# The retention state loop of a hybrid decoder step: four value-row buffers, another order of DMAs, constants behind two weight slots

## The reference

```python
def retention_chunk(S, q, k, v, log_gamma):      # for a sample: L = 1
    ...
    cross = jnp.einsum('bihd,bhdv->bihv', q * q_dec[None, :, :, None], S)
    ...
    S_new = jnp.exp(L * log_gamma)[None, :, None, None] * S + jnp.einsum('bjhd,bjhv->bhdv', k * k_dec[None, :, :, None], v)
    return inner + cross, S_new
```

## Time and profile before

| | |
|---|---|
| median of 3 runs | 1556.37 us (1551.08 to 1560.65) |
| the profiled execution | 1557.63 us, its span 1555.7 us |
| TensorE busy | 1378.6 us, 89% of the span |
| VectorE busy | 636.5 us, 41% |
| ScalarE busy | 248.1 us, 16% |
| POOL busy | 122.0 us, 8% |
| granted TensorE clock, mean | 0.91 of full speed |

### The profile page before, as it was taken

One profiled execution on the slowest core, in us unless ns is written; L12 is line 12 of the kernel. 1 busy time (PEld: TensorE's weight loads), 2 busy tenths in 40 slices (PEclk: granted clock), 3 DMA queues, 4 the chain that ended last, 5 costly groups with the idle time before them and its releaser, 6 DMA issues.

```text
span 1555.7 us, 19005 instructions
## 1 busy us (share of the span) xinstructions
PE 1378.6 (89%) x6290; PEld 753.3 (48%) x6290; DVE 636.5 (41%) x1681; ACT 248.1 (16%) x518; POOL 122.0 (8%) x234
## 2 busy tenths in 40 slices
PE   6899876789998999999899969988888889999995
PEld 4687544567864443334577723322324644334343
DVE  2132334320025444444400087787781243535354
ACT  2001224312013000000210021221221130000001
POOL 3331223210000000000000001111110000000000
PEclk9899978899999999999899956686799989999998
DMA  9764848686566999999953346666663639999992
GB/s 373 296 232 151 287 175 258 238 267 264 194 275 234 388 402 399 401 408 406 396 214 128 136 157 214 220 244 229 234 240 136 237 142 353 407 393 416 400 405 111
DMA packets 77033, 430.16 MB, mean 277 GB/s; under 512 B 9833, under 2 KB 11129, under 8 KB 38433
## 3 DMA queue, kind: packets, MB, share of 16 engines
q1 hardware_dynamic: 52704, 347.72, 57.1%
q0 software_dynamic: 23200, 76.10, 14.6%
q10 hardware_dynamic: 1056, 5.36, 0.9%
HBM read 406.94 MB, written 22.20 MB: 276 GB/s over the span
## 4 chain that ended last, share of the span: by engine, by line
PE 69%; DMA 14%; DVE 9%; issue 3%; ACT 2%; DVEq 1%; POOL 1%; SPq 0%; POOLq 0%; ACTq 0%
PE bank L802 66%; DMA ring<-wstream 7%; DMA xn<-v_rows 4%; DMA arena<-state 2%; DVE arena L2163 1%; DVE arena L1999 1%; DVE h L2159 1%; PE bank L858 1%; DVE x L2015 1%; DVEq L1994 1%; DVE arena L1721 1%; ACT arena L1530 1%; ACT xn L1418 1%; DVE arena L2028 1%; POOL ss_out L715 0%
## 5 line engine op out<-in xcount | busy, mean ns | idle before, releaser
L802 PE MATMUL bank<-arena 128*128 128x264 f32 (+7 forms) x1216 | 407.0, 526 | 60.4 <-DVE arena L1721 32.2
L802 PE MATMUL bank<-ring,arena 128*64 128x512 f32 (+3 forms) x1856 | 393.0, 558 | 9.1 <-issue 5.8
L802 PEld LDWEIGHTS bank<-arena 128*128 128x128 f32 (+4 forms) x1216 | 171.7, 169 | 275.4 <-issue 169.0
L802 PEld LDWEIGHTS bank<-ring,arena 128*64 128x64 f32 (+3 forms) x1856 | 141.7, 137 | 240.6 <-issue 208.1
L1400 ACT ACTIVATE arena<-bank 128x256 f32<-128x256 f32 (+6 forms) x186 | 87.0, 472 | 555.6 <-PE bank L802 456.4
L802 PE MATMUL bank<-h,ring 128*128 128x264 f32 x640 | 149.0, 395 | 6.3 <-DMA ring<-wstream 6.3
L802 PEld LDWEIGHTS bank<-h,ring 128*128 128x128 f32 x640 | 123.9, 195 | 32.5 <-issue 11.1
L2015 DVE SCALAR_TENSOR_TENSOR x<-bank,mod,x 128x256 f32<-128x256 f32 x256 | 119.2, 472 | 0.0
L802 PE MATMUL bank<-arena,ring 128*128 128x264 f32 x512 | 116.3, 390 | 0.8 <-DVE arena L2242 0.8
L802 PE MATMUL bank<-arena,cst 16*128 16x128 f32 (+8 forms) x210 | 78.1, 481 | 32.9 <-DVE arena L2224 20.3
L802 PEld LDWEIGHTS bank<-arena,ring 128*128 128x128 f32 x512 | 98.2, 192 | 18.3 <-DVE arena L2242 0.9
(11 more groups left out here) (229 smaller groups left out, 868.2 us busy)
## 6 DMA issues: line engine op xcount, KB each, us to landing
ring<-wstream SPq DMA_DIRECT2D x296, 1024.0 KB, 8.7
arena<-vcache POOLq DMA_DIRECT2D x64, 512.0 KB, 5.6
arena<-kcache SPq DMA_DIRECT2D x64, 512.0 KB, 4.7
arena<-state POOLq DMA_DIRECT2D x32, 512.0 KB, 8.8
ss_out<-arena POOLq DMA_DIRECT2D x32, 512.0 KB, 7.7
xn<-v_rows POOLq DMA_DIRECT2D x32, 256.0 KB, 7.7
sp_out<-arena ACTq DMA_DIRECT2D x4, 512.0 KB, 2.9
cst<-consts SPq DMA_DIRECT2D x1, 2005.5 KB, 16.4
```

The source lines that it names most:

```text
L802: ins = nc.tensor.matmul(out, w, rhs, start=start, stop=stop, skip_group_check=True)
```

## The change

- The value rows get a fourth buffer. The four now take 2048 of the columns of `xn` from its start; `vpart`, which lay there, moves to `sp_sb`.
- POOL's loop goes pair by pair. It waits until VectorE has moved pair p, spreads the rows of units 2p + 4 and 2p + 5, waits until TensorE has read the pair, stores its two units, and loads the states of units 2p + 3 and 2p + 4 (where these are 7 or more). The next head's values are stored after the second of four pairs, as before.
- ScalarE scales pairs in that order: sample_rows(0) takes the place of scale_pair(5) behind v column 7; in head hd the two scalings are of pairs 5 + 2hd and 6 + 2hd (they were 6 + 2hd and 7 + 2hd); sample_rows(2) stands in front of the second scaling of head 3 and not behind it; pairs 13, 14 and 15 follow g columns 0, 1 and 2 (14 and 15 followed columns 0 and 1).
- SyncE loads slots 12 and 13, the first two of q, before the rest of the constants.
- POOL's first seven state loads wait for VectorE's first rotated q column and not for the first row of m0b.

```diff
@@ -376,7 +376,6 @@
         ret = Region(0)
         qk = ret.take(2 * KT, T)
         vtok = ret.take(2, RH * RV)
-        vpart = xn[:, :, :].rearrange("p a b -> p (a b)")[:, 0:RV]
         qz = ret.take(2, RH, NS * NS)
         oret = ret.take(RVT, T)
         gsil = ret.take(2, 2, T)
@@ -386,12 +385,13 @@
         at_sb = ret.take(2, 3 * P)
         ktok = ret.take(2, 2, RK)
         sp_sb = ret.take(2, RV)
+        vpart = sp_sb.rearrange("p a b -> p (a b)")[:, 0:RV]
         sq_s = ktok.rearrange("p a b c -> p (a b c)")[:, 0:RVT * NS].rearrange("p (t b) -> p t b", t=RVT)
         rot = ret.take(4, T)
         osb = rot.rearrange("p a b -> p (a b)")[:, RV:2 * RV]
         root_o = ret.take(1, TP)
         vr = rot.rearrange("p a b -> p (a b)")[:, 0:RV]
-        vb = xn[:, :, :].rearrange("p a b -> p (a b)")[:, RV:4 * RV].rearrange("p (r n) -> p r n", r=3)
+        vb = xn[:, :, :].rearrange("p a b -> p (a b)")[:, 0:4 * RV].rearrange("p (r n) -> p r n", r=4)
         squares = gsil.rearrange("p a b n -> p (a b) n")[:, :, 0:TP]
         hs = oret.rearrange("p a b -> p (a b)")[:, 2304:2304 + KT * MW].rearrange("p (k n) -> p k n", k=KT)
 
@@ -517,7 +517,7 @@
         sam_rooted = sem("sam_rooted")
         sam_ready = sem("sam_ready")
         v_stored = sem("v_stored")
-        vb_in = [sem(f"vb_in{r}") for r in range(3)]
+        vb_in = [sem(f"vb_in{r}") for r in range(4)]
         state_moved = sem("state_moved")
         state_scaled = sem("state_scaled")
         state_read = sem("state_read")
@@ -654,11 +654,11 @@
                 sp.dma_start(kpg[:, j % 4, :], kcache[ds(page, 1)].rearrange("a p n -> p (a n)")) \
                     .then_inc(k_in[j % 4], 16)
 
-            for n in range(R, S_RET):
+            for n in range(R, S_RET + 2):
                 sp.wait_ge(slot_used, n - R + 1)
                 sp.dma_start(ring[:, n % R, :], wstream[n]).then_inc(slot_in[n % R], 16)
             rest_of_constants()
-            stream(S_RET, S_MOE0 + 3 * NE)
+            stream(S_RET + 2, S_MOE0 + 3 * NE)
 
             sp.wait_ge(ids_in, 16)
             for r in range(SB):
@@ -689,7 +689,7 @@
 
                 return u % NS * RH + u // NS
 
-            moved(pool, ("row", "m0b", 0))
+            moved(pool, ("qk", 0, 0))
             for u in range(SB):
                 pool.dma_start(st[:, u, :, :], state[state_of(u)]).then_inc(state_in[u], 16)
 
@@ -700,27 +700,36 @@
             def values_everywhere(u):
                 if u % NS == 0:
                     pool.wait_ge(v_stored, 16 * (u // NS + 1))
-                pool.dma_start(vb[:, u % 3, :], v_rows[u // NS, u % NS:u % NS + 1, :].to_broadcast([P, RV])) \
-                    .then_inc(vb_in[u % 3], 16)
+                pool.dma_start(vb[:, u % 4, :], v_rows[u // NS, u % NS:u % NS + 1, :].to_broadcast([P, RV])) \
+                    .then_inc(vb_in[u % 4], 16)
+
+            def load_state(u):
+                if u < NS * RH:
+                    pool.wait_ge(state_out[u % SB], 16 * (u // SB))
+                    pool.dma_start(st[:, u % SB, :, :], state[state_of(u)]).then_inc(state_in[u % SB], 16)
 
             store_values(0)
-            for u in range(3):
+            for u in range(4):
                 values_everywhere(u)
-            for u in range(NS * RH):
-
-                if u // 2 % 4 == 3:
-                    result(pool, ("os", u // NS))
+            for p in range(NS * RH // 2):
+
+                pool.wait_ge(state_moved, 2 * p + 2)
+                if p < NS * RH // 2 - 2:
+                    values_everywhere(2 * p + 4)
+                    values_everywhere(2 * p + 5)
+                if p % 4 == 3:
+                    result(pool, ("os", p // 4))
                 else:
-                    pool.wait_ge(state_read, 3 * (u // NS) + u // 2 % 4 + 1)
-                pool.dma_start(ss_out[state_of(u)], st[:, u % SB, :, :]).then_inc(state_out[u % SB], 16)
-                if u + 3 < NS * RH:
-                    values_everywhere(u + 3)
-                nxt = u + 5
-                if SB <= nxt < NS * RH:
-                    pool.wait_ge(state_out[nxt % SB], 16 * (nxt // SB))
-                    pool.dma_start(st[:, nxt % SB, :, :], state[state_of(nxt)]).then_inc(state_in[nxt % SB], 16)
-                if u % NS == 3 and u // NS + 1 < RH:
-                    store_values(u // NS + 1)
+                    pool.wait_ge(state_read, 3 * (p // 4) + p % 4 + 1)
+                for u in (2 * p, 2 * p + 1):
+                    pool.dma_start(ss_out[state_of(u)], st[:, u % SB, :, :]).then_inc(state_out[u % SB], 16)
+                if p == 0:
+                    continue
+                for u in (2 * p + 3, 2 * p + 4):
+                    if u >= SB:
+                        load_state(u)
+                if p % 4 == 1 and p // 4 + 1 < RH:
+                    store_values(p // 4 + 1)
 
             def page_of(j):
                 return pool.value_load(page_ids[0:1, ds(j, 1)], min_val=0, max_val=kcache.shape[0] - 1)
@@ -1451,9 +1460,10 @@
                 for c in range(2):
                     ps = result(act, ("v", i, c))
                     copy(vtok[:, c, i * 256:(i + 1) * 256], ps[:, 0:256]).then_inc(free(("v", i, c)), 1)
-                if i >= 2:
+                if i == 7:
+                    sample_rows(0)
+                elif i >= 2:
                     scale_pair(i - 2)
-            sample_rows(0)
             for hd in range(RH):
                 for v in range(4):
                     ps = result(act, ("ro", hd, v))
@@ -1465,7 +1475,7 @@
                 for s in range(2):
                     ps = result(act, ("rs", hd, s))
                     copy(sp_sb[:, s, :], ps[:]).then_inc(free(("rs", hd, s)), 1)
-                scale_pair(6 + 2 * hd)
+                scale_pair(5 + 2 * hd)
                 moved(act, ("rs", hd, 1))
                 act.dma_start(sp_out[hd], sp_sb).then_inc(sp_stored, 16)
                 if hd:
@@ -1473,8 +1483,9 @@
                 head_root(hd)
                 if hd == 1:
                     sample_rows(1)
-                scale_pair(7 + 2 * hd)
-            sample_rows(2)
+                if hd == 3:
+                    sample_rows(2)
+                scale_pair(6 + 2 * hd)
 
             for i in range(8):
                 if i >= 2:
@@ -1482,8 +1493,8 @@
                 for m in range(2):
                     ps = result(act, ("g", i, m))
                     nc.scalar.activation(gsil[:, i % 2, m, :], ps[:, 0:T], ACT.Silu).then_inc(free(("g", i, m)), 1)
-                if i < 2:
-                    scale_pair(14 + i)
+                if i < 3:
+                    scale_pair(13 + i)
                 if i == 3:
                     sample_rows(3)
                 if i == 5:
@@ -1715,10 +1726,10 @@
             def move_states(p):
                 for u in (2 * p, 2 * p + 1):
                     hd, b = u // NS, u % NS
-                    dve.wait_ge(vb_in[u % 3], 16 * (u // 3 + 1))
+                    dve.wait_ge(vb_in[u % 4], 16 * (u // 4 + 1))
                     dve.wait_ge(state_scaled, u + 1)
                     for s in range(2):
-                        ins = stt(st[:, u % SB, s, :], vb[:, u % 3, :], qk[:, 8 + 2 * hd + s, TP + b:TP + b + 1],
+                        ins = stt(st[:, u % SB, s, :], vb[:, u % 4, :], qk[:, 8 + 2 * hd + s, TP + b:TP + b + 1],
                                   st[:, u % SB, s, :], ALU.mult, ALU.add)
                     ins.then_inc(state_moved, 1)
 
```

## The result

The changed kernel takes 1591.37 us, median of 4 runs (1588.41 to 1601.21), against 1558.51 for the kernel before beside it on the same chip: ratio 1.0225, interval 1.0189 to 1.026. So it is slower, by 23 to 33 us by the medians; whether by more than two per cent, the two sets leave open. 15 us was forecast.

What follows compares the result with a forecast made beforehand. The prediction took TensorE to bound most of the chain, with DMA (value rows 4%, states 2%) the part the change touches. Its terms summed to +15.0 us, 1571 against 1556.4; the 8 in 10 range was 1548 to 1586.

Steps and rivals of the forecast that it cites:

- opening: Start of the q columns: with two slots ahead of the constants, TensorE starts at 43.85 us, 6.3 us earlier.
- V columns, pairs 1 and 2: TensorE's idle before these reads goes because value rows come two pairs early: 2.9 us gained.
- V columns, pairs 3 and 4: Pair 3 comes 0.8 us sooner, pair 4, waiting for load 9, 0.4 later: together 0.4 us gained.
- first pair of a head: Pairs 5, 7, 9, 11: the read waits for two scalings and a move behind the `rs` copies, 17.0 us lost.
- second pair of a head: Pairs 6, 8, 10: waiting for the later load, each takes 13.0 us in place of 10.5, 6.9 us lost.
- pair 12: Gate columns: 5.54 us of idle goes as sample rows precede scaling; 13.9 us for 20.5, 6.6 gained.
- pairs 13 to 15: Gate columns: these take 40.3 us where they took 33.0, waiting for late loads, 7.3 us lost.
- rival 4: The opening does not pay: constants late by more than 4 us, up to 6.3 us back, 1577 us; chance 0.05.
- Landing of the load: POOL's first state load behind a pair lands at t + 8.5 in the heads, 10.5 beside a weight slot.
- rival 1: Loads land early, near t + 6.4, deciding from t + 6.8 downward: 1553 us or down to 1547; chance 0.20.
- rival 2: Loads land late, t + 10 in heads and t + 12 beside a slot: 1584 us; chance 0.15.
- rival 3: The first pair of a head is not held, ScalarE's new place costs nothing: 17.0 us less, 1554; chance 0.08.

Runs made afterwards that it cites:

- e14: The changed kernel once more, unaltered: 1586.15 us against 1563.34 for the kernel before, ratio 1.0157.
- e9: The kernel before with each value row transfer reading 128 different rows of the weight stream instead of one row 128 times: 1553.15 us in one execution.
- e8: The kernel before, unaltered, run for a second profile: 1549.72 us in its one execution.
- e13: The changed kernel with ScalarE's scaling places as in the kernel before, loads left late: 1611.65 us, ratio 1.0324.
- e6: The changed kernel with the next head's values stored ahead of the pair's two state stores instead of behind them: 1583.05 us, ratio 1.0151.
- e2: The changed kernel with loads of units 2p+5 and 2p+6 and ScalarE's earlier scaling order, sample rows still ahead of their scaling: 1523.45 us, ratio 0.9746.
- e4: The changed kernel with the constants back in front of slot 12: 1591.2 us, ratio 1.0226.
- e15: An unaltered copy of e4, the changed kernel with the constants in front of slot 12: 1592.75 us.
- e10: The kernel before with the constants behind two q slots, SyncE's weight loop laps kept as before: 1555.24 us, ratio 0.9974.

## Why the prediction missed, step by step

The direction in the stage, and the mechanism named as the one that decides (the load issued one pair later), were right; the size was not. t is when TensorE has read a pair. Between the same points of the two profiles (the last read ends at 339.78 before and at 363.88 after):

| step | predicted | profile |
|---|---|---|
| opening | -6.3 | -5.8 at the q columns, -4.5 at the read of pair 0 |
| V columns, pairs 1 and 2 | -2.9 | -2.3 |
| V columns, pairs 3 and 4 | -0.4 | +4.8 |
| first pair of a head (5, 7, 9, 11) | +17.0 | +16.8 (1.9, 4.8, 5.2, 4.9) |
| second pair of a head (6, 8, 10) | +6.9 | +6.2 |
| pair 12 | -6.6 | -7.0 |
| pairs 13 to 15 | +7.3 | +10.0 |
| sum | +15.0 | +24.0 |

The 9 us between the two sums are 5.2 from pairs 3 and 4, 2.7 from the last three pairs and 1.8 from the opening; the rest nearly cancels. The median stands 20 us over the 1571 forecast: these 9, 2 by which the median of the kernel before came out higher than in the runs that I had, and some 9 that only this set of runs shows and e14 does not.

**Opening: right where it starts.** The q columns start at 44.31 for 50.12, against 43.9 forecast. At the end of the program the medians favour the gain without settling it, so rival 4 (it does not pay) is unlikely but not out. By pair 0 this profile has lost 1.3 us of it: the read at 142.74 waits 1.89 us for 0.91 before, and runs 1.63 us for 1.04. The fourth row transfer ahead of it does not explain this, since e14, the same kernel, shows 0.96 and 1.04 at that read; it is scatter of single profiles.

**Rows leave the path: right**, and worth little, as the step said: pairs 1 and 2 gain 2.3.

**Landing of the load.** I took t + 8.5 in the heads. The first load behind t = 221.19 was issued at 222.54 and landed 6.43 us later, t + 7.8; in the next two heads it was t + 9.0, where POOL came 0.75 us late, and t + 7.9. This lies between the forecast and rival 1, which needed t + 6.8. Rival 1 and rival 2 (t + 10) are both out in the heads. The way to 8.5 was not right: the count had a trough of 3 us in it, and the trough is gone (197 GB/s at the least, see e9 above). That was the premise of rival 1, but the load gained only 0.7 us by it. In the gate columns, beside a slot, it was t + 9.9 (issued 322.21, 8.56) for 10. By the Trainium skill, page "DMA: Bandwidth & Descriptors", section "Anatomy of one DMA — SWDGE (gpsimd) path", a formula for one DMA, about 2.0 us plus bytes over 436 GB/s, taken over the bytes of the queue gave the estimate t + 5.8; the measured t + 7.8 disagrees by 2 us, less than for the shorter queue before (t + 8.9 for t + 5.3).

**First pair of a head: the idle right, the sum right by luck, its meaning wrong.** 17.0 was forecast and 16.8 measured, the 4.5 us of idle are where I put them, and rival 3 is out. But pair 5 came 1.9 us later and not 4.6, and pair 9 5.2 and not 3.6. Pair 5's small loss is due to the profile I compared with: from pair 4 to pair 5 it took 21.3 us, since the clock stayed at 1.2 GHz until about 214 us; e8, the same program, took 16.3. The windows of before and of e8:

```profile
205.00:210.00 5.00, 4.62 (x18) 3.96 (x18) 1.69 (x5) 0.00 (x0) 0.00 (x0) 0.50 0.91 349
```

```profile
205.00:210.00 5.00, 4.26 (x31) 3.83 (x30) 2.66 (x9) 0.00 (x0) 0.00 (x0) 1.00 0.80 256
```

Against e8 pair 5 would stand at +6.9 and the stage end 28 us later, not 24. I also booked the step as the price of an edit to ScalarE's order beside the late loads. e13 shows it as part of them: with that edit undone the kernel loses 25 us more.

**V columns, pair 3: the step that failed.** "Pair 3 read at t(2) + 12.4 (load 7 at + 8.7, since its rows went out early)". It was read at t(2) + 17.2. POOL's rows for pair 4 had not gone out early: they stand behind the stored values, which land 7.5 us after their issue behind two 512 KB stores. So pair 2's stores leave 1.6 us behind t(2) (165.74 for 164.12; 0.28 is usual), and the load, beside a weight slot, takes another 9.9: it landed at t(2) + 12.6, not + 8.7. I had asked what is queued behind POOL's wait for the move, and not what is queued behind its wait for `v_stored`, which the new order puts ahead of the stores. e6 parts the 3.9 us: without the stall the load lands at t(2) + 10.6 (issued 164.35, 9.2 us, t(2) at 162.95), so 2.0 are the stall. The other 1.9 are the weight slot, for which my own rule had 10.5; I left it out here, because the rows were to be early.

**Gate columns: pair 12 right, 13 to 15 too small by 2.7.** Gaps of 14.5 and 14.9 for 14.6 are right; the last was 13.5 for 11.1. I let the last pair's load go faster since no value rows come before it; its queue still held a weight slot (8.19 us from issue to landing).

**Behind the stage.** I booked nothing, and no run shows a cost there: 24 us by the profile, 23 and 33 in two sets of medians. The spread between the two is wider than any of my small terms, and a sum made against one profiled execution cannot be told from the truth closer than that.

**What tells right from wrong** in the signs I had listed: q columns at 43.9 (44.3), VectorE's row waits all but gone (one is left, 7.7 us at pair 0), ScalarE's waits for states over 70 (72.6), stores in the heads 12.4 to 12.8 and 15.0 to 16.9 us apart, idle of 3.7 to 4.5 us ahead of each first read, no 5.5 us in the gate columns: all came out. The range ended at 1586, since its upper end rested on late landings everywhere (rival 2, 1584) and on nothing for a stall of POOL in one place.

## What to carry to other kernels

When one of two loads leaves the critical loop, write down the chain of the other one with all its steps; here a load issued one pair later took the row's place and brought a scaling with it. Ordering work by the queue that issues it is sound (e2: the same four buffers and early rows, loads as early as before, 36 us faster than the kernel before; the opening and the new place of the sample rows are in these 36, and no run has the rows' order by itself), but the prefetch distance must not shrink with it: the number in that one line was worth 40 us. An in-order engine that works ahead needs its inputs still further ahead, or it holds everything behind it; and for every wait that is moved, not only for the one that the change speaks of, list what stands behind it on the engine.

## What the runs showed of the hardware

Two copies of one program differed by 5 us (the changed kernel and e14) and two of another by 11.6 us (e4 and e15) in the stretch of some 1110 us behind the same mark, and the 23 executions of the kernel before beside e10 spread from 1550.61 to 1568.03. Nine profiles fell in two clean groups by an edit, and repeats of the same programs did not keep to them. The clock is one thing that varies: behind pair 4 it was at 0.50 from 205 to 210 us in one profile of the kernel before and at 1.00 in another.

A 16 KB store behind two 512 KB stores in POOL's queue took 7.5 us to land (issue at 156.61); issued ahead of such stores, in e6 at 154.30, it took 1.8. A transfer of 256 KB in 2 KB pieces, second in its queue behind a store, landed in 6.3 to 6.4 us whether its source was one row or 128 of them. With a store ahead, the queue had a stretch of some 3 us down to 37 GB/s; with two such transfers first it had none under 197 once it ran.
